# The modulation weights of a hybrid block, loaded along the contraction and multiplied as columns

## What is computed

```python
c_act = jax.nn.silu(c)
mod = c_act @ w_ada[l] + b_ada[l]
sh1, sc1, gt1, sh2, sc2, gt2 = jnp.split(mod, 6, axis=-1)
u = _rmsnorm(h, g_mix[l]) * (1 + sc1) + sh1
proj = u @ w_in          # q, k, v, us, two gates
...                      # attention, state space branch, merge, w_out
...                      # feed-forward block; then the second layer and a last norm
```

## Time and profile before

| what | value |
|---|---|
| median of three runs | 2168.71 us (2168.64 to 2171.28) |
| the profiled execution | 2168.5 us, of which the span of the profile is 2166.8 us |
| PE busy | 2133.2 us, 98% of the span |
| DVE, ACT, POOL busy | 790.8, 411.1 and 1047.5 us |
| first product with `w_in` (L751) begins | 56.74 us into the span |

### The profile page before, as it was taken

One profiled execution on the slowest core, in us unless ns is written; L12 is line 12 of the kernel. 1 busy time (PEld: TensorE's weight loads), 2 busy tenths in 40 slices (PEclk: granted clock), 3 DMA queues, 4 the chain that ended last, 5 costly groups with the idle time before them and its releaser, 6 DMA issues.

```text
span 2166.8 us, 25663 instructions
## 1 busy us (share of the span) xinstructions
PE 2133.2 (98%) x10574; PEld 1780.7 (82%) x10574; DVE 790.8 (36%) x1100; ACT 411.1 (19%) x593; POOL 1047.5 (48%) x452
## 2 busy tenths in 40 slices
PE   7999999999999999999999999999999999999998
PEld 3788888888888888888888798888888888888888
DVE  6961355555553621222212665310032111241143
ACT  3302232323321310201101221111010110110203
POOL 1537446645363546445454445334545355536461
PEclk9999999999999999999999999999999999999999
DMA  9455545453552102011020231102111011111131
GB/s 348 119 108 155 195 130 158 142 174 100 183 187 66 39 30 88 20 59 48 29 78 30 69 126 59 39 30 68 58 40 48 31 58 50 47 39 49 48 126 78
DMA packets 157119, 192.30 MB, mean 89 GB/s; under 512 B 11152, under 2 KB 138720, under 8 KB 157024
## 3 DMA queue, kind: packets, MB, share of 16 engines
q1 hardware_dynamic: 148096, 172.05, 25.4%
q10 hardware_dynamic: 8928, 18.88, 2.3%
HBM read 159.20 MB, written 31.70 MB: 88 GB/s over the span
## 4 chain that ended last, share of the span: by engine, by line
PE 95%; DVE 2%; POOL 1%; DMA 1%; issue 0%; SPq 0%; ACT 0%; DVEq 0%; POOLq 0%; ACTq 0%
PE ps L727 64%; PE ps L803 8%; PE ps L751 7%; PE ps L1025 3%; PE ps L1194 2%; PE ps L761 2%; PE ps L986 2%; PE ps L916 1%; PE ps L1000 1%; PE ps L1337 1%; POOL w_h L648 1%; DMA ada_w<-in_w_ada 1%; PE ps L1256 1%; POOL w_l L650 1%; DVE acc L2187 0%
## 5 line engine op out<-in xcount | busy, mean ns | idle before, releaser
L648 POOL TENSOR_SCALAR w_h<-raw 128x1024 fp32r<-128x1024 f32 (+2 forms) x202 | 506.4, 2507 | 914.1 <-PE ps L727 628.9
L727 PE MATMUL ps<-act_h,w_h 128*128 128x512 f32 x1600 | 625.8, 391 | 0.9 <-POOL w_l L650 0.5
L727 PE MATMUL ps<-act_l,w_h 128*128 128x512 f32 x1600 | 623.1, 389 | 0.0
L727 PE MATMUL ps<-act_h,w_l 128*128 128x512 f32 x1600 | 623.1, 389 | 0.0
L650 POOL TENSOR_TENSOR w_l<-raw,w_h 128x1024 fp32r<-128x1024 f32 (+2 forms) x202 | 436.9, 2163 | 16.9
L727 PEld LDWEIGHTS ps<-act_h,w_h 128*128 128x128 f32 x1600 | 300.8, 188 | 67.0 <-issue 2.9
L727 PEld LDWEIGHTS ps<-act_h,w_l 128*128 128x128 f32 x1600 | 300.7, 188 | 62.8
L727 PEld LDWEIGHTS ps<-act_l,w_h 128*128 128x128 f32 x1600 | 300.8, 188 | 62.2 <-issue 0.5
L727 PE MATMUL ps<-in_h,w_h 128*128 128x512 f32 x384 | 150.0, 391 | 0.9 <-POOL w_l L650 0.9
L727 PE MATMUL ps<-in_l,w_h 128*128 128x512 f32 x384 | 149.4, 389 | 0.0
L727 PE MATMUL ps<-in_h,w_l 128*128 128x512 f32 x384 | 149.4, 389 | 0.0
(11 more groups left out here) (351 smaller groups left out, 2874.2 us busy)
## 6 DMA issues: line engine op xcount, KB each, us to landing
raw<-in_w_in SPq DMA_DIRECT2D x45, 1024.0 KB, 5.3
raw<-in_w_up SPq DMA_DIRECT2D x16, 1024.0 KB, 5.4
ada_w<-in_w_ada SPq DMA_DIRECT2D x8, 1024.0 KB, 11.9
ada_lo<-in_w_ada SPq DMA_DIRECT2D x16, 512.0 KB, 3.8
ada_hi<-in_w_ada SPq DMA_DIRECT2D x16, 512.0 KB, 4.8
gates_scratch<-gate_st ACTq DMA_DIRECT2D x32, 256.0 KB, 2.3
gate_in<-gates_scratch SPq DMA_DIRECT2D x16, 512.0 KB, 4.4
raw<-in_w_down SPq DMA_DIRECT2D x16, 512.0 KB, 3.4
```

What stands on the lines that cost most here:

```text
L648: nc.gpsimd.tensor_scalar(w_h[:, k, c, :], src[:, c, :], 1.0, None, ALU.mult).then_inc(s["w_high"], 1)
L727: last = nc.tensor.matmul(dst[:, tok], w[:, k, kw + c, P * cg:P * cg + P], x[:, c, tok], start=(c == 0 and p == 0), stop=(c == kc - 1 and ...
```

## The change

The first 2048 columns of `w_ada` are loaded in five parts along the contraction: chunks 0 and 1, 2 and 3, 4 and 5, 6, and 7, each with all 2048 columns. Where a DMA fetched pieces of 256 neighbouring values, it now fetches 2048. The first block of `w_in` comes after the second part instead of after the first pair.

On PE the rows are gone. For each chunk and each of 12 groups of 128 outputs, the new `ada_columns` holds 128 by 128 weights in the array and streams one column of `c_act` past them: 96 products of one column, which add up in place, already as columns. The other four groups (512 outputs) are summed over the chunks by DVE in five pieces, strewn between its other work, and PE adds them over the partitions with four products as before. ACT's three copies of rows are gone.

The vector `c` is loaded by its own small DMA ahead of `x` and transposed first, and ACT makes `c_act` before anything else. The square root of the norms moves ahead of ACT's exponentials and sines, and the reciprocal and the diagonal move ahead on DVE. The transposes of `rows` move behind the first `ada_columns` on PE, and the copies to `cols_a` and `cols_b`, with all that DVE does behind them, follow them. DVE's table of powers moves behind `norm`. The first chunk is normalised in two halves of 512 tokens, and PE begins it with the first half.

```diff
@@ -43,7 +43,9 @@
 N_V2, N_A, N_GA, N_B, N_GB, N_C, N_GC, N_WO, N_END = 55, 57, 61, 69, 77, 85, 89, 97, 101
 N_ADA_EARLY, N_ADA = 8, 24
 SUMMED = 1
-ROWS = N_ADA_EARLY // 2 - SUMMED
+ADA_PARTS = ((0, 2), (2, 4), (4, 6), (6, 7), (7, 8))
+ADA_PE = 12
+ADA_DONE = 3
...
-        ada_w = at("ada_w", [P, N_ADA_EARLY, KD, NB], 0)
+        ada_w = at("ada_w", [P, KD, N_ADA_EARLY * NB], 0)
+        ada_sum = at("ada_sum", [P, N_ADA_EARLY * NB - ADA_PE * P], 204 * kib)
...
+            sp.dma_start(c_row[:], a["c"].flatten().rearrange("(r p) -> r p", p=P)).then_inc(c_in, 16)
             for t in range(0, QB, 2):
...
-            def ada_pair(i):
-                for b in (2 * i, 2 * i + 1):
-                    sp.dma_start(ada_w[:, b, :, :], weights("w_ada", bass.ds(b * NB, NB))).then_inc(ada0_in[i], 16)
+            def ada_part_in(i):
+                lo, hi = ADA_PARTS[i]
+                sp.dma_start(ada_w[:, lo:hi, :], weights("w_ada", slice(0, N_ADA_EARLY * NB), row=lo * P, k=hi - lo))\
+                  .then_inc(ada0_in[i], 16)
 
...
-            ada_pair(0)
+            for i in range(2):
+                ada_part_in(i)
             first(0, 3 * ATT)
-            for i in range(1, N_ADA_EARLY // 2):
-                ada_pair(i)
+            for i in range(2, len(ADA_PARTS)):
+                ada_part_in(i)
             first(1, 0)
...
+            def product_pair(slots, k, kc, high, low, ready, base=0, split=None, head=None):
...
-                        if c == kc - 1:
+                    by_half = head is not None and c == 0
+                    if by_half:
+                        pe.wait_ge(head, 3)
+                    else:
+                        pe.wait_ge(ready, base + (c + 1))
+                    for i in range(4):
+                        cg, th = (i % 2, i // 2) if by_half else (i // 2, i % 2)
+                        if by_half and i == 2:
+                            pe.wait_ge(ready, 1)
+                        tok = slice(HALF * th, HALF * th + HALF)
+                        for p, (w, x) in enumerate(((w_h, high), (w_h, low), (w_l, high))):
+                            last = nc.tensor.matmul(slot(slots[cg])[:, tok], w[:, k, c, P * cg:P * cg + P], x[:, c, tok],
+                                                    start=(c == 0 and p == 0), stop=(c == kc - 1 and p == 2),
+                                                    skip_group_check=True)
+                        if c == kc - 1 and i % 2:
                             last.then_inc(s["gemm"], 1)
...
             pe.wait_ge(s["const_in"], 16)
+            pe.wait_ge(c_in, 16)
+            nc.tensor.transpose(slot(3)[:, 0:KD], c_row[:], ident[0:KD, 0:KD]).then_inc(s["colt"], 1)
             for t in range(QB):
                 pe.wait_ge(x_in[t // 2], 16)
+                if t == 3:
+                    pe.wait_ge(s["c_ready"], 1)
...
-            pe.wait_ge(s["vec_in"], 16 * (len(ROWS_A) + len(ROWS_B)))
-            pe.wait_ge(s["h_ready"], QB)
-            nc.tensor.transpose(slot(3)[:, 0:P], rows[:, 0, :], ident[:])
-            nc.tensor.transpose(slot(3)[:, P:P + n_b], rows[0:n_b, 1, :], ident[0:n_b, 0:n_b]).then_inc(s["colt"], 1)
...
+            def ada_columns(i):
+
+                pe.wait_ge(ada0_in[i], 16)
+                for c in range(*ADA_PARTS[i]):
+                    for b in range(ADA_PE):
+                        last = nc.tensor.matmul(slot(2)[:, b:b + 1], ada_w[:, c, P * b:P * b + P], c_act[:, c:c + 1],
+                                                start=(c == 0 and b == 0), stop=(c == KD - 1), skip_group_check=True)
+                return last
...
-            def ada_row(i):
-
-                pe.wait_ge(ada0_in[i], 32)
-                dst = row_place(i).rearrange("p (b n) -> p b n", b=2)
-                for c in range(KD):
-                    last = nc.tensor.matmul(dst, c_act[:, c:c + 1], ada_w[:, 2 * i:2 * i + 2, c, :],
-                                            start=(c == 0), stop=(c == KD - 1))
-                last.then_inc(s["ada_row"], 1)
...
-            def ada_columns(i):
-
-                if i < ROWS:
-                    pe.wait_ge(s["row_copied"], i + 1)
-                else:
-                    pe.wait_ge(s["ada_summed"], i - ROWS + 1)
-                for b in (2 * i, 2 * i + 1):
-                    dst = slot(2)[:, 2 * b:2 * b + 2]
-                    if i >= ROWS:
-                        last = ada(dst, ada_w[:, b, 0, :])
-                    else:
-                        for cg in range(2):
-                            last = nc.tensor.matmul(dst[:, cg:cg + 1], ada_w[0:1, b, 0, P * cg:P * cg + P], ones[0:1, 0:1],
-                                                    start=True, stop=True)
-                    last.then_inc(s["ada_done"], 1)
...
-            for i in range(ROWS):
-                ada_row(i)
-                if i:
-                    ada_columns(i - 1)
+            pe.wait_ge(s["h_ready"], QB - 1)
+            ada_columns(0)
+            pe.wait_ge(s["vec_in"], 16 * (len(ROWS_A) + len(ROWS_B)))
+            pe.wait_ge(s["h_ready"], QB)
+            nc.tensor.transpose(slot(3)[:, 0:P], rows[:, 0, :], ident[:])
+            nc.tensor.transpose(slot(3)[:, P:P + n_b], rows[0:n_b, 1, :], ident[0:n_b, 0:n_b]).then_inc(s["colt"], 1)
+            ada_columns(1)
+            pe.wait_ge(s["colt_read"], 1)
             for th in range(2):
                 spread = everywhere(1, slot(3)[:, HALF * th:HALF * th + HALF], diag[:, 4 * th:4 * th + 4])
             spread.then_inc(s["rstd_ready"], 1)
-            ada_columns(ROWS - 1)
-            ada_columns(ROWS)
-
-
-            product_pair((0, 1), 0, KD, act_h, act_l, s["u_ready"], split=0)
+            for i in range(2, len(ADA_PARTS)):
+                last = ada_columns(i)
+            last.then_inc(s["ada_done"], 1)
+            pe.wait_ge(s["ada_summed"], 1)
+            for b in range(ADA_PE, 2 * N_ADA_EARLY, 2):
+                ada(slot(1)[:, b:b + 2], ada_sum[:, P * (b - ADA_PE):P * (b - ADA_PE) + NB]).then_inc(s["ada_done"], 1)
+
...
+            product_pair((0, 1), 0, KD, act_h, act_l, s["u_ready"], split=0, head=s["head0"])
...
+            act.wait_ge(s["colt"], 1)
+            A.activation(c_act[:], slot(3)[:, 0:KD], ACT.Silu).then_inc(s["c_ready"], 1)
...
-            act.wait_ge(s["colt_read"], 1)
-            A.activation(c_act[:], col_a("c", 0, KD), ACT.Silu).then_inc(s["c_ready"], 1)
+            act.wait_ge(s["consts_ready"], 3)
+            A.activation(stat[:, 0, :], stat[:, 2, :], ACT.Sqrt, scale=1.0 / D, bias=eps_rms[:]).then_inc(s["std_ready"], 1)
...
-            act.wait_ge(s["consts_ready"], 3)
-            A.activation(stat[:, 0, :], stat[:, 2, :], ACT.Sqrt, scale=1.0 / D, bias=eps_rms[:]).then_inc(s["std_ready"], 1)
...
-            def row(i):
-
-                act.wait_ge(s["ada_row"], i + 1)
-                A.activation(ada_w[0:1, 2 * i:2 * i + 2, 0, :],
-                             slot(i // 2)[0:1, HALF * (i % 2):HALF * (i % 2) + 2 * NB].rearrange("p (b n) -> p b n", b=2),
-                             ACT.Copy).then_inc(s["row_copied"], 1)
...
-            norm_high(0, slice(0, T), lambda i: nrm[:, i, :], lambda c: mod[:, c:c + 1])
+            act.wait_ge(s["head0"], 1)
+            A.activation(act_h[:, 0, 0:HALF], nrm[:, 0, 0:HALF], ACT.Identity, bias=mod[:, 0:1]).then_inc(s["head0"], 1)
+            norm_high(0, slice(0, T), lambda i: nrm[:, i, :], lambda c: mod[:, c:c + 1], first=slice(HALF, T))
...
-            dve.wait_ge(s["colt"], 1)
+            dve.wait_ge(s["colt"], 2)
             step(v.tensor_copy(cols_a[:], slot(3)[:, 0:P]))
             v.tensor_copy(cols_b[:, 0:n_b], slot(3)[:, P:P + n_b]).then_inc(s["colt_read"], 1)
             dve.wait_ge(s["colt_read"], 1)
...
+            def ada_early(i):
+                dve.wait_ge(ada0_in[i], 16)
+                ada_sums(ada_sum[:], lambda c: ada_w[:, c, ADA_PE * P:], range(*ADA_PARTS[i]))
+
+            one_over_root(1)
+            on_diagonal(diag[:], stat[:, 1, :])
+            dve.wait_ge(s["c_ready"], 1)
+            ada_early(0)
...
@@ -1775,6 +1804,7 @@
...
+            ada_early(1)
...
             v.tensor_scalar(comp, comp, np.pi / 2, None, ALU.add).then_inc(s["s5_dve"], 1)
+            ada_early(2)
             dve.wait_ge(s["s5_act"], S5_ACT["turn_ready"])
...
-            def ada_early(i):
-                dve.wait_ge(ada0_in[i], 32)
-                ada_sums(ada_w[:, 2 * i:2 * i + 2, 0, :], lambda c: ada_w[:, 2 * i:2 * i + 2, c, :])
...
-            one_over_root(1)
-            on_diagonal(diag[:], stat[:, 1, :])
...
-            ones_first(power)
-            for i in range(LOGC):
-                doubled(power, 2**i, lambda m, i=i: step_turn[:, m, :, i])
-            step(v.tensor_copy(power[:, :, :, CHUNK], step_turn[:, :, :, LOGC]))
-            dve.wait_ge(s["c_ready"], 1)
-            for i in range(SUMMED):
-                ada_early(ROWS + i)
-            dve.wait_ge(s["ada_done"], N_ADA_EARLY)
```

(22 more changed lines are left out.)

88 lines of the change are left out of this document (42 added, 46 removed).

## The result

The changed kernel takes 2181.18 us, the median of five runs (2179.77 to 2184.07), against 2168.64 us for the kernel before beside it (2165.93 to 2171.28). The ratio is 1.0062, 95% interval 1.0047 to 1.0077: slower by 12.5 us. The profiled execution was the slowest of the five: it took 2184.07 us with a span of 2182.3, which is 15.5 us longer than the span before.

What follows compares the result with a forecast made beforehand. The prediction took PE to bound the kernel, with the start of `norm` setting the rest. That start 17.8 us later, nothing from the halves, on 2168.5 gave 2186.3, adjusted to 2186.5 us; range 2180.5 to 2190.

Steps and rivals of the forecast that it cites:

- First weights: Loading of `w_ada`: larger pieces land 1.0 us earlier, so PE starts its columns at 21.6 instead of 22.63 us.
- The clock stays at 0.50 in the columns: PE's 96 one-column products: all expected at clock 0.50, 1.2 instead of 2.4 GHz; this case was given 0.53.
- The rival that continuous work holds the clock: PE's columns: gapless work keeps 2.4 GHz, so the change is not slower, 2167.5 us; chance 0.12.
- Loads slow with the clock: PE's weight loads: taken to double at clock 0.50; the rival that they do not, 2167.5 us, had 0.03.
- Price of an instruction: PE's columns: 192 instructions at 0.223 us each at clock 0.50, 42.8 us in all.
- Other work of PE: PE beside the columns: transposes of `rows` 0.5, spreading of the norms 3.5, last four products with tail 1.9 us.
- N: Time at which DVE begins `norm`: 52.75 us before, forecast 70.5, which is 17.8 later.
- The spreading lifts the clock: Rival: the wide spreading of norms among PE's columns restores full clock for a while, saving 3.4 us, 2183.1; chance 0.28.
- DVE's chain hidden: DVE's copies and sums behind the transposes of `rows`: 22.5 us, ending at 55.3, hidden behind PE's 68.4.
- The halves are worth nothing: First chunk in halves: PE starts 1.7 us earlier but waits 2 to 3 for POOL's second block; no gain.
- The power table is only hidden: DVE's 3.1 us table behind `norm`: hidden by a 2.65 us wait; at most 0.5 shows, PE does not wait.
- A delay of N is a delay of the end: PE never runs short of work, so a delay or gain at its first `w_in` product reaches the end.

Runs made afterwards that it cites:

- experiment 1: Changed kernel with the two products that spread the norms moved behind all 96 one-column products: 2184.81 us, 1.0071 of the kernel before.
- experiment 2: Changed kernel with the 96 one-column products made 24 products of 512 columns again: 2168.84 us, 0.9999 of the kernel before.
- 3: Changed kernel with the first chunk normalised whole, as before the change: 2184.57 us, 1.0064 of the kernel before.
- 4: Changed kernel with DVE's table of powers ahead of `norm` again: 2184.21 us, 1.0067 of the kernel before.
- 5: Kernel before with only the first chunk normalised in halves, power table still ahead of `norm`: 2171.24 us, 1.0006 of the kernel before.
- 6: Kernel before with the first chunk in halves and the power table behind `norm`: 2164.82 us, 0.9980 of the kernel before.

## Why the prediction was right, and where not

The direction, the main mechanism and the range held: 2181.2 in 2180.5 to 2190.0, 0.7 above its lower end, forecast 2186.5. By its steps:

- **First weights**: 21.6 forecast; PE began the columns at 21.81, and at 21.6 to 21.7 in experiments 1 to 4.
- **The clock stays at 0.50 in the columns**: right, but for the lift of 3.4 us below, and shown by experiment 2 against 1. The rival that continuous work holds the clock fell. The Trainium skill, "TensorE: Matmul & The Clock Gate", section "Why this matters for your kernels", taken by the letter, would have kept it; PE was busy for 14.10 of 14.10 us at 0.50.
- **Loads slow with the clock**: right. Loads of one and the same line L915 took 334 ns at 0.50, and 192 ns later in the program at 1.00 (rows below). The same page's section "LDWEIGHTS (loading the stationary operand)" has no term for the clock, and the trace does not agree with it.
- **Price of an instruction**: 0.223 forecast, 0.213 measured. 192 of them took 40.9 us where no lift came (experiment 1), not 42.3 (42.8 less the 0.5 taken off): 1.4 too much.
- **Other work of PE**: the spreading 3.5 forecast, 3.55 where the clock was 0.50 throughout (62.90 to 66.45 in experiment 1) and 3.18 in the changed kernel, where the clock rose inside it. The last four products with their tail 1.7 instead of 1.9, the transposes 0.4 instead of 0.5: 0.3 too much. With the columns that is 1.6 too much in N, which is 68.86 in experiment 1 and not 70.5.
- **The spreading lifts the clock**: a rival with 0.28, and it did in the profiled execution, worth 2.9. It did in two of the four traces that have the spreading among the columns, so neither case alone is the answer; for the profiled execution this rival is right and my forecast isn't. N is 65.9 with the lift and 68.9 without.
- **DVE's chain hidden**: right. It ended at 53.7 (forecast 55.3), 9.7 us before PE needed its sums.
- **The halves are worth nothing**: right by themselves (4 and 5), wrong with the table moved (1.4 us, 3). **The power table is only hidden**: this step failed. I took POOL's 14.0 us as fixed, while they depended on what DVE did beside them. They became 11.5, and the two edits together gave 2.1 us (6). PE's wait for POOL was 0.7, not 2 to 3, for the same reason, and no further fall of the clock came there.
- **A delay of N is a delay of the end**: right to the fifth chunk. Behind it the clock adds up to 4.5 us of its own in one execution; of no edit is it shown that it controls this. In experiment 1, 2.9 us more of N left no trace in the end.

For the profiled execution the account closes. The forecast was 17.8 us more than before, and the fifth chunk came only 11.0 later. The 6.7 in between are the lift, 2.9, the prices on PE, 1.65, and POOL's shorter split with the halves, 2.1. The clock behind the chunk then added 4.5, which the sum had put at nothing, and it ended 15.5 later. That these 4.5 us stood against the 6.7 is luck. The miss of 5.3 us between the forecast and the median can't be shared out in this way, since four of its five executions have no trace.

The loads of L915 in the changed kernel: the group from 63 to 66 us (busy us, mean ns), and then those of 281 us and later (least, median and longest ns).

```profile
L915 PEld LDWEIGHTS ps<-ones,ada_sum 128*128 128x128 f32 x8 | 1.8, 334 | 0.0
```

```profile
L915 PEld LDWEIGHTS ps<-ones,ada_part x64: 191/192/193, 281.5 to 570.1; 128*128 128x128 f32 x64
```
